# Gate and up projections as seven block products, ffn tiles in passes of 12 and 10, in a two-layer decoder step

## The chip, the cores and the metric

The kernel runs on one core of one Trainium2 chip. The metric is the device time of one execution in microseconds (us), the median of the runs shown. Engines are PE (TensorE, the matmuls), PEld (its weight loads), DVE (VectorE), ACT (ScalarE), POOL (GpSimd) and SP (SyncE, which issues loads).

## The reference

One step of a decoder of two layers over 520 tokens (a prompt of 512 and eight sequences of one new token), all in fp32. Each layer has a mixer (layer 0 gated linear recurrence and pooling, layer 1 retention), a residual add, and the feed-forward network (ffn) that this case is about; a last norm follows. D_MODEL is 1024, D_FF 2816.

```python
def rms_norm(x, gain=None):
    y = x32 * lax.rsqrt(jnp.mean(x32 * x32, axis=-1, keepdims=True) + EPS)
    ...
def swiglu(h, w_gate, w_up, w_down):
    return (jax.nn.silu(h @ w_gate) * (h @ w_up)) @ w_down
...
        x = x + y
        x = x + swiglu(rms_norm(x, norm_ffn[i]), w_ffn_gate[i], w_ffn_up[i], w_ffn_down[i])
    return rms_norm(x, norm_final), ...
```

## The kernel before

Activations lie transposed: `x` is 128 partitions by 8 k-tiles by 520 tokens, and every projection makes one 128x520 tile of outputs in PSUM, as two halves of 260 tokens. TensorE multiplies in a rounded fp32 format, so each fp32 factor is split into a rounded part (hi) and the rest (lo), and a product is three matmuls: hi times hi, hi times lo and lo times hi. ScalarE makes hi by a copy with rounding (`hi` L351, `h_hi` L360), VectorE makes lo by a subtraction (`lo` L706, `h_lo` L711).

Per layer the ffn has 22 tiles of 128 hidden units. Each tile is one load of 1 MB (weights of gate and up, 128x2048), and two products of 48 matmuls (8 k-tiles, 3 splits, 2 halves), gate and up, through two alternating PSUM tiles `ps`. VectorE evicts both with a multiplication by `rstd`, the rms-norm's factor per token (L722 into `t0` and `t2`); ScalarE makes silu (L476); VectorE multiplies (L958), makes the next weights' lo (L706) and the lo of the hidden tile (L961); ScalarE its hi (L480). After all 22 come eight down tiles of 132 matmuls (two loads of 11 k-tiles each), added to `x` by one VectorE instruction each (`residual`, L722). In layer 0 each is followed by `h_lo` (L711) for the next projection. The squares for the next norm are GpSimd's (L1236, L1238); TensorE sums them over partitions (`norm_sum`, L1379) and spreads the factor (`norm_spread`, L1387), in the first tile of the phase that follows.

The order on each engine is written out by hand, in one program for each, tied by counting semaphores: `wait_ge(s, n)` holds an engine's queue until a count is reached. The long stretches are hardware loops over two tiles. SP loads a chunk when the hi and lo of two chunks before are done.

The last down tile of the kernel runs half by half (L1862), 66 matmuls each, and the final norm of the first half (`last_squares`, `y_sum` L1843, `y_spread` L1852, six outputs L1214) is put inside and behind the second:

```python
                    if t == 1 and n == Y_AFTER[0]:
                        y_sum(0)
                    if t == 1 and n == Y_AFTER[1]:
                        y_spread(0)
```

## Time and profile before

| | before |
|---|---|
| median of 3 runs | 1501.72 us (1501.26 to 1503.73) |
| profiled execution, span | 1500.0 us |
| PE busy | 1469.1 us (98%), 11754 matmuls |
| DVE busy | 728.8 us (49%) |
| ACT busy | 475.5 us (32%) |
| POOL busy | 208.4 us (14%) |
| share of the chain that ended last: PE, DVE | 95%, 2% |

The span is one execution by the hardware profiler, from its first instruction to its last. A time in the chain is a stretch of work that nothing but itself held up. "Idle" is the time an engine stood still ahead of an instruction, with what released it.

### The profile page before, as it was taken

What the parts mean: (1) busy time and instruction counts of PE and PEld (TensorE: products, weight loads), DVE (VectorE), ACT (ScalarE), POOL (GpSimd) and SP (SyncE); (2) the same over time, 40 slices, a digit from 0 to 9 for tenths busy, and PEclk for the clock granted to TensorE, in tenths of its full rate; (3) what the DMA queues carried; (4) which work ended last, traced back from release to release, by engine and by line L of the source; (5) the groups of instructions that cost most, each with busy time, mean ns of one, the idle gap of its engine ahead of it and who ended that gap; (6) DMA issues with size and microseconds to landing.
All of it is one profiled execution on the core that took longest, in us unless ns stands there. A gap on an engine that the chain in (4) does not pass through costs nothing.

```text
span 1500.0 us, 28016 instructions
## 1 busy us (share of the span) xinstructions
PE 1469.1 (98%) x11754; PEld 1426.6 (95%) x11754; DVE 728.8 (49%) x867; ACT 475.5 (32%) x547; POOL 208.4 (14%) x209
## 2 busy tenths in 40 slices
PE   6999999999999999999999999989999999999997
PEld 5989999999999999988989989979999999999997
DVE  6564544444443333465574773875444444443223
ACT  3432232222222212254263362463222222221111
POOL 6011130000000112014013041041210000000221
PEclk9999999999999999999999999999999999999998
DMA  6212122222222222555254263333222222222221
GB/s 236 85 61 93 54 88 85 84 97 99 84 75 77 95 97 90 219 175 183 85 204 154 98 232 111 140 140 142 85 99 99 84 84 98 97 66 78 96 97 57
DMA packets 32230, 165.84 MB, mean 111 GB/s; under 512 B 3904, under 2 KB 6224, under 8 KB 20400
## 3 DMA queue, kind: packets, MB, share of 16 engines
q1 hardware_dynamic: 21792, 126.90, 24.3%
q0 software_dynamic: 10384, 38.16, 7.1%
q8 instruction: 40, 0.66, 0.2%
q14 instruction: 14, 0.11, 0.0%
HBM read 140.46 MB, written 24.59 MB: 110 GB/s over the span
## 4 chain that ended last, share of the span: by engine, by line
PE 95%; DVE 2%; ACT 1%; POOL 1%; issue 0%; DMA 0%; DVEq 0%; SPq 0%; ACTq 0%; POOLq 0%
PE ps L1361 83%; PE ax L1722 2%; PE ax L1731 1%; PE ax L1704 1%; PE ps L1862 1%; PE ax L1651 1%; PE ax L1743 1%; PE ax L1379 1%; PE ax L1387 1%; DVE h_lo L711 1%; PE ax L1689 0%; PE ax L1530 0%; POOL acc L1233 0%; PE ax L1499 0%; DMA x<-in_x 0%
## 5 line engine op out<-in xcount | busy, mean ns | idle before, releaser
L1361 PE MATMUL ps<-h_hi,whi 128*128 128x260 f32 x2432 | 496.8, 285 | 1.3 <-DVE wlo L731 1.3
L1361 PE MATMUL ps<-h_hi,wlo 128*128 128x260 f32 x2432 | 491.1, 284 | 0.0
L1361 PE MATMUL ps<-h_lo,whi 128*128 128x260 f32 x2432 | 490.1, 283 | 0.0
L1361 PEld LDWEIGHTS ps<-h_hi,whi 128*128 128x128 f32 x2432 | 376.4, 189 | 8.0 <-issue 4.9
L1361 PEld LDWEIGHTS ps<-h_hi,wlo 128*128 128x128 f32 x2432 | 375.9, 189 | 0.0
L1361 PEld LDWEIGHTS ps<-h_lo,whi 128*128 128x128 f32 x2432 | 375.4, 189 | 0.0
L351 ACT ACTIVATE whi<-raw 128x2048 fp32r<-128x2048 f32 (+1 forms) x119 | 210.6, 1770 | 490.4 <-PE ps L1361 481.9
L706 DVE TENSOR_TENSOR wlo<-raw,whi 128x2048 fp32r<-128x2048 f32 (+1 forms) x119 | 255.5, 2147 | 128.9 <-ACT whi L351 128.7
L722 DVE TENSOR_TENSOR t<-ps,rstd 128x520 f32<-128x520 f32 x108 | 75.5, 699 | 274.8 <-PE ps L1361 269.1
L1361 PE MATMUL ps<-hid_hi,whi 128*128 128x260 f32 x660 | 133.2, 283 | 0.0
L1361 PE MATMUL ps<-hid_hi,wlo 128*128 128x260 f32 x660 | 132.7, 282 | 0.0
L1361 PE MATMUL ps<-hid_lo,whi 128*128 128x260 f32 x660 | 132.6, 282 | 0.0
L1361 PEld LDWEIGHTS ps<-hid_lo,whi 128*128 128x128 f32 x660 | 101.9, 188 | 0.0
L1361 PEld LDWEIGHTS ps<-hid_hi,wlo 128*128 128x128 f32 x660 | 101.7, 188 | 0.0
L1361 PEld LDWEIGHTS ps<-hid_hi,whi 128*128 128x128 f32 x660 | 101.6, 188 | 0.0
L1229 POOL TENSOR_TENSOR acc<-x 128x520 f32<-128x520 f32 x5 | 5.8, 1162 | 593.2 <-DVE x L722 538.9
L476 ACT ACTIVATE t<-t 128x520 f32<-128x520 f32 x44 | 28.2, 640 | 171.9 <-DVE t L722 171.9
L722 DVE TENSOR_TENSOR x<-ps,x 128x520 f32 (+1 forms) x31 | 21.7, 699 | 120.6 <-PE ps L1361 120.4
L1236 POOL TENSOR_TENSOR sq<-x 128x520 f32<-128x520 f32 x32 | 35.7, 1114 | 242.2 <-DVE x L722 241.5
L360 ACT ACTIVATE h_hi<-x,vec 128x520 fp32r<-128x520 f32 (+1 forms) x32 | 22.7, 726 | 126.5 <-DVE x L722 124.9
L1238 POOL TENSOR_TENSOR acc<-acc,sq 128x520 f32<-128x520 f32 x32 | 61.0, 1907 | 2.5
L1361 PE MATMUL ps<-o_hi,whi 128*128 128x260 f32 x256 | 52.7, 288 | 6.6 <-issue 2.9
(260 smaller groups left out, 1587.6 us busy)
## 6 DMA issues: line engine op xcount, KB each, us to landing
raw<-in_w_f SPq DMA_DIRECT2D x44, 1024.0 KB, 4.7
...
```

The costliest lines, as they stand in the source:

```text
L351: act.activation(whi[slot][:, 0:size], raw[slot][:, 0:size], ACT.Copy).then_inc(s_whi, 1)
L360: act.activation(flat(h[0], m), flat(x, m), ACT.Copy, scale=gain(n, m)).then_inc(s_hhi, 1)
L476: act.activation(t1[:], t0[:], ACT.Silu).then_inc(s_sg, 1)
L706: dve.tensor_tensor(wlo[slot][:, 0:size], raw[slot][:, 0:size], whi[slot][:, 0:size].bitcast(F32), ALU.subtract).then_inc(s_wlo, 1)
L711: dve.scalar_tensor_tensor(out=flat(h[1], m), in0=flat(x, m), scalar=gain(n, m), in1=flat(h[0], m).bitcast(F32), op0=ALU.mult, op1=ALU.sub ...
L722: dve.tensor_tensor(out, ps[par][:, :, 0:HT], two(rstd) if other is None else other, op).then_inc(s_out, 1)
L1236: pool.tensor_tensor(sq[:], x[:, m, :], x[:, m, :], ALU.mult).then_inc(s_sq, 1)
L1238: pool.tensor_tensor(acc[:], acc[:], sq[:], ALU.add).then_inc(s_acc, 1)
L1361: ins = pe.matmul(dst[t], lhs(a, kw), rhs[b][:, kx, HT * t:HT * t + HT], start=(first and n == 0 and q == 0), stop=(last and n == len(ks_) ...
L1379: ins = pe.matmul(ax[3][:, col + i:col + i + 1], src[:, a:a + P], ones[:, 0:1], start=True, stop=True)
L1387: ins = pe.matmul(dst, rr[:, rcol + i:rcol + i + 1].to_broadcast([P, P]), ident[:, c:c + n], start=True, stop=True)
L1722: ins = pe.matmul(ax[q % 2][:, P * j:NP_], v[:, j, P * q:P * q + P], p_[:, PROB_AT[j]:PROB_AT[j + 1]], start=(j == 0 and n == 0), stop=(j ...
```

## The change

Gate and up of one ffn tile are now a product of a 2x2 matrix of blocks with another: the rows are up (first) and gate (second), the columns of the right factor are the two halves of 260 tokens, and the inner dimension is cut into the even and the odd k-tiles. Winograd's form of Strassen's scheme needs seven block products for it, of four k-tiles, three splits and one half each, 12 matmuls (`f_product`), so 84 matmuls a tile. It needs four sums of weight blocks (S1 to S4, per tile) and four of activations (T1 to T4, once per layer, in `hx`, split into `hs`), and seven additions behind the products, of which TensorE's accumulation in PSUM does some. The sums of a tile:

- VectorE: `f_sum_13` (S1 and S3, 128x1024), `f_sum_2` (128x512), `f_sum_4` (128x512), lo of three parts (1536, 1024, 1024), `up_first`, `up_second`, `gate_second` (128x260 each, from PSUM), `gate_first_scaled` and `gate_second_scaled` (128x260, by rstd with the sign), `hidden` and `hid_low` (128x520).
- ScalarE: hi of the same three parts (1536, 1024, 1024), three copies of 128x260 out of PSUM, silu, the hidden tile's hi.

rstd is applied to gate alone ahead of silu; up's factor is left to the down projection, whose tiles are evicted by two instructions (`down_taken`: a multiplication by rstd, L1249, and the add to `x`, L1252, with other VectorE work, `inside`, between). The hidden tensor holds 12 tiles in place of 22, so the ffn has two passes: 12 tiles and eight down tiles of 72 matmuls, then 10 tiles and eight of 60. The sums and splits of `hx` are built pair by pair in the out-projection ahead of the ffn. `norm_sum` stands behind P6 and `norm_spread` behind P7 of the first tile. The last down tile has 30 matmuls a half. Some semaphores of loads and of heads share a number with others now.

```diff
-W_FULL, W_HALF, W_DOWN = 2048, 1024, 11 * P
+W_FULL, W_HALF = 2048, 1024
+FH = (12, 10)
+W_DOWN = (FH[0] * P, FH[1] * P)
+F0 = (0, FH[0])
...
+A11, A12, A22, S1, S2, S3, S4 = range(7)
+F_BLOCK = ({A22: 0, A11: 1, A12: 2, S4: 4, S2: 5, S1: 6, S3: 7}, {A12: 1, A11: 2, A22: 3, S2: 4, S4: 5, S3: 6, S1: 7})
+
+F_RAW = ({"A22": 0, "A11": 1, "A12": 2, "A21": 3}, {"A21": 0, "A12": 1, "A11": 2, "A22": 3})
+B11, T1, B21, B22, T2, T3, T4 = range(7)
...
+            def f_hi_s24(g, q, free):
+                act.wait_ge(f_s4, g + 1)
+                act.wait_ge(*free)
+                act.activation(fw[0][:, 4:6, :], fraw[q][:, raw_sums(q), :], ACT.Copy).then_inc(s_whi, 1)
+
...
+                def period(n, q, first=False, final=False):
+                    f_hi_s24(g0 + n, q, (s_mm, before) if first else (f_p3, g0 + n))
+                    if first and half == 0:
+                        act.wait_ge(s_tlo, 12 * (l + 1))
+                    copies_1(n, q)
+                    if first and half == 0:
+                        copies_5(n, q)
+                        copies_6(n, q)
+                        act.wait_ge(s_ms, 2 * l + 2)
+                        act.activation(rt[:, 0:5], ax[3][:, 64:69], ACT.Sqrt, bias=eps[:, 0:1]).then_inc(s_rt, 1)
+                    if final:
+                        act.wait_ge(f_p2, g0 + n + 1)
+                        hi(cd, 0, W_DOWN[half], (f_p4, g0 + n))
+                    else:
+                        f_hi_raw(g0 + n + 1, 1 - q, c0 + n + 1,
+                                 [(f_p2, g0 + n + 1)] + ([] if first else [(f_p4, g0 + n)]))
+                    if not (first and half == 0):
+                        copies_6(n, q)
+                    if not first:
+                        silu(n - 1, 1 - q)
+                    if not (first and half == 0):
+                        copies_5(n, q)
+                    else:
+                        act.wait_ge(s_bc, 2 * l + 2)
+                        act.activation(rstd[:, 0:NP_], ax[2][:], ACT.Copy)
+                        act.activation(rstd[:, NP_:T], ax[3][:, 72:72 + NS], ACT.Copy).then_inc(s_rstd, 1)
+                    if not first:
+                        hid_high(n - 1)
+                    if not final:
+                        f_hi_s13(g0 + n + 1, (f_p7, g0 + n + 1))
+
+                if half == 1:
+                    f_hi_s13(g0, (s_mm, before))
...
+            def hx_sum(sn, j, part):
+
+                n = 4 * sn + j
+                if part == 0:
+                    dve.wait_ge(s_hx, 2 * n + 1)
+                    dve.tensor_tensor(hx[:, T1, :], hx[:, B11, :], hx[:, 7, :], ALU.subtract).then_inc(s_tsum, 1)
+                else:
+                    dve.wait_ge(s_hx, 2 * n + 2)
+                    dve.tensor_tensor(hx[:, T3, :], hx[:, B22, :], hx[:, 7, :], ALU.subtract).then_inc(s_tsum, 1)
+                    dve.wait_ge(s_tsum, 4 * n + 1)
+                    dve.scalar_tensor_tensor(out=hx[:, T2, :], in0=hx[:, B22, :], scalar=-1.0, in1=hx[:, T1, :],
+                                             op0=ALU.mult, op1=ALU.subtract).then_inc(s_tsum, 1)
+                    dve.wait_ge(s_tsum, 4 * n + 3)
+                    dve.scalar_tensor_tensor(out=hx[:, T4, :], in0=hx[:, T2, :], scalar=-1.0, in1=hx[:, B21, :],
+                                             op0=ALU.mult, op1=ALU.subtract).then_inc(s_tsum, 1)
...
+            def f_lo_raw(g, q):
+                dve.wait_ge(f_ha, g + 1)
+                a = raw_triple(q)
+                dve.tensor_tensor(fw[1][:, a, :], fraw[q][:, a, :], fw[0][:, a, :].bitcast(F32), ALU.subtract).then_inc(f_la, 1)
+
...
+                def period(n, q, first=False, final=False):
+                    if not (first and half == 0):
+                        f_lo_s13(g0 + n)
+                    if not first:
+                        up_second(n - 1, 1 - q)
+                    f_lo_s24(q, c0 + n)
+                    if not final:
+                        f_sum_13(g0 + n + 1, 1 - q, c0 + n + 1)
+                        f_sum_2(g0 + n + 1, 1 - q)
+                    if not first:
+                        gate_first_scaled(n - 1, 1 - q)
+                    up_first(n, q)
+                    if first and half == 0:
+                        invert(2 * l + 1)
+                    if final:
+                        lo(cd, 0, W_DOWN[half])
+                    else:
+                        f_lo_raw(g0 + n + 1, 1 - q)
+                        f_sum_4(g0 + n + 1, 1 - q)
+                    if not first:
+                        hidden(n - 1, 1 - q)
+                    gate_second(n, q)
+                    if not first:
+                        hid_low(n - 1)
+                    if first and half == 0:
+                        dve.wait_ge(s_rstd, 2 * l + 2)
+                    gate_second_scaled(n, q)
...
+            def down_taken(l, half, m, q, inside):
+
+                dm = M_D[l][half]
+                dve.wait_ge(s_mm, dm + m + 1)
+                want(dve, s_xd, 16 * l + 8 * half + m)
+                dve.tensor_tensor(two(t1), ps[(dm + q) % 2][:, :, 0:HT], two(rstd), ALU.mult).then_inc(s_out, 1)
+                inside()
+                dve.wait_ge(s_out, dm + m + 1)
+                dve.tensor_tensor(flat(x, m), t1[:], flat(x, m), ALU.add).then_inc(s_xd, 1)
...
+                def tile_(m, q):
+                    down_taken(l, half, m, q, lambda: lo(d0 + m + 2, q, size))
+                    if (l, half) == (0, 1):
+                        h_lo(2, m)
...
+                if half == 0:
+                    def first_sums():
+                        f_sum_13(g1, 0, C_F[l][1])
+                        f_sum_2(g1, 0)
+
+                    def first_raw():
+                        f_lo_raw(g1, 0)
+                        f_sum_4(g1, 0)
+
+                    down_taken(l, half, 6, 0, first_sums)
+                    down_taken(l, half, 7, 1, first_raw)
+                elif l == 0:
+                    for m in (6, 7):
+                        down_taken(l, half, m, m % 2, lambda: lo(C_OI + m - 6, m - 6, W_FULL))
+                        h_lo(2, m)
+                else:
...
+                def f_product(block, moving, bank, start, done, ready=None):
+
+                    for j in range(4):
+                        if ready is not None:
+                            pe.wait_ge(s_tlo, 12 * l + 3 * j + ready)
+                        for n, (a, b) in enumerate(((0, 0), (0, 1), (1, 0))):
+                            ins = pe.matmul(bank, fw[a][:, block, P * j:P * j + P], hs[b][:, j, moving, :],
+                                            start=(start and j == 0 and n == 0), stop=(j == 3 and n == 2),
+                                            skip_group_check=True)
+                    ins.then_inc(done, 1)
+
+                def product_4(n, q):
+                    pe.wait_ge(f_g1, g0 + n + 1)
+                    f_product(F_BLOCK[q][A22], T4, bank_a(q), False, f_p4)
...
+                def chunk(n, q, first=False):
+                    blocks, g = F_BLOCK[q], g0 + n
+                    early = first and half == 0
+
+                    def product_5():
+                        pe.wait_ge(f_lb, g + 1)
+                        want(pe, f_u1, g - 1)
+                        f_product(blocks[S1], T1, bank_d(q), True, f_p5, 1 if early else None)
+
+                    pe.wait_ge(f_la, g + 1)
+                    if first:
+                        pe.wait_ge(s_out, before - 1)
+                    want(pe, f_gr, 2 * g - 2)
+                    f_product(blocks[A11], B11, bank_a(q), True, f_p1, 1 if early else None)
+                    if early:
+                        product_5()
+                    want(pe, f_u0, g - 1)
+                    f_product(blocks[A12], B21, bank_e(q), True, f_p2, 2 if early else None)
+                    if not first:
+                        product_4(n - 1, 1 - q)
+                    pe.wait_ge(s_wlo, c0 + n + 1)
+                    pe.wait_ge(f_k1, g + 1)
+                    f_product(blocks[S2], T2, bank_a(q), False, f_p6, 3 if early else None)
+                    if early:
+                        norm_sum(2 * l + 1)
+                    else:
+                        product_5()
+                    pe.wait_ge(f_k6, g + 1)
+                    f_product(blocks[S3], T3, bank_a(q), False, f_p7)
+                    if early:
+                        norm_spread(2 * l + 1)
+                    pe.wait_ge(f_k5, g + 1)
+                    f_product(blocks[S4], B22, bank_d(q), False, f_p3)
+
+                chunk(0, 0, first=True)
+                pe.wait_ge(s_out, before)
+                with pe.Fori(0, last // 2) as i:
+                    chunk(2 * i + 1, 1)
+                    chunk(2 * i + 2, 0)
+                chunk(last, 1)
...
-                for n in range(FT):
-                    if n % 11 == 0:
-                        pe.wait_ge(s_wlo, C_D[1] + N_D - 1 + n // 11)
+                for n in range(FH[1]):```

VectorE's queue in the loop over gate/up tiles, before: one tile (t_62 to t_65 are t0 to t3, the number behind wlo, raw and whi is a buffer; what is waited for stands in brackets).

```order
L721 ISA [waits silu_gate]
L722 TENSOR_TENSOR t_62<-ps,rstd 128x520 [waits mtile_done]
L721 REGISTER_ALU
L722 TENSOR_TENSOR t_64<-ps,rstd 128x520 [waits mtile_done]
L956 REGISTER_ALU [waits mtile_taken]
L958 TENSOR_TENSOR t_65<-t_64,t_63 128x520 [waits hidden_hi,silu_gate]
L705 REGISTER_ALU
L706 TENSOR_TENSOR wlo_53<-raw_49,whi_51 128x2048 [waits weights_hi]
L961 ISA [waits hidden_hi]
L961 TENSOR_TENSOR hid_lo<-t_65,hid_hi 128x520
```

The same queue and place in the change: the last ten of one tile's thirteen instructions, behind L1137, L1176 and L1141 (f_lo of S1 and S3, `up_second`, f_lo of S2 and S4).

```order
L1115 TENSOR_TENSOR f_sum<-f_raw_75 128x1024 [waits ffn_s1_s3_lo,raw1_loaded]
L1120 REGISTER_ALU
L1121 TENSOR_TENSOR f_raw_75<-f_sum,f_raw_75 128x512 [waits ffn_s1_s3_summed]
L1191 SCALAR_TENSOR_TENSOR rs<-ps,rstd 128x260 [waits ffn_product4]
L1171 TENSOR_TENSOR t_64<-ax,t_64 128x260 [waits ffn_product1_copied,ffn_product2]
L1133 TENSOR_TENSOR f_lo<-f_raw_75,f_hi 128x1536 [waits ffn_raw_hi]
L1128 TENSOR_TENSOR f_raw_75<-f_raw_75 128x512 [waits ffn_raw_lo]
L1199 TENSOR_TENSOR t_65<-t_63,sq 128x520 [waits ffn_up_second,hidden_hi,ffn_up_first,silu_gate]
L1181 TENSOR_TENSOR t_62<-ps,t_62 128x260 [waits ffn_product5_copied,ffn_product7]
L1203 ISA [waits hidden_hi]
L1203 TENSOR_TENSOR hid_lo<-t_65,hid_hi 128x520
L1186 SCALAR_TENSOR_TENSOR t_62<-t_62,rstd 128x260 [waits ffn_gate_second]
```

Five instructions of a tile became thirteen. L1121 and L1128 wait for the instruction that stands right ahead of them; L1203 waits for ScalarE's copy of what L1199 made, two instructions before.

VectorE's queue at the end of the first pass, in the change: the last two down tiles of it and the first weights of the second pass. There is no such place before.

```order
L1249 TENSOR_TENSOR t_63<-ps,rstd 128x520 [waits x_after_down,mtile_done]
L1115 TENSOR_TENSOR f_sum<-f_raw_74 128x1024 [waits ffn_s1_s3_lo,raw0_loaded]
L1121 TENSOR_TENSOR f_raw_74<-f_sum,f_raw_74 128x512 [waits ffn_s1_s3_summed]
L1252 TENSOR_TENSOR x<-t_63,x 128x520 [waits mtile_taken]
L1249 TENSOR_TENSOR t_63<-ps,rstd 128x520 [waits x_after_down,mtile_done]
L1133 TENSOR_TENSOR f_lo<-f_raw_74,f_hi 128x1536 [waits ffn_raw_hi]
L1128 TENSOR_TENSOR f_raw_74<-f_raw_74 128x512 [waits ffn_raw_lo]
L1252 TENSOR_TENSOR x<-t_63,x 128x520 [waits mtile_taken]
L1137 TENSOR_TENSOR f_lo<-f_sum,f_hi 128x1024 [waits ffn_s1_s3_hi]
L1141 TENSOR_TENSOR f_lo<-f_raw_74,f_hi 128x1024 [waits weights_hi]
```

The lo that the second pass's first product needs (L1133) stands behind the eviction of the pass's last down tile (the second L1249).

VectorE's queue at the end of layer 0, before: the last down tile, with weights for layer 1's projection around it.

```order
L706 TENSOR_TENSOR wlo_53<-raw_49,whi_51 128x2048 [waits weights_hi]
L722 TENSOR_TENSOR x<-ps,x 128x520 [waits mtile_done]
L711 SCALAR_TENSOR_TENSOR h_lo<-x,vec,h_hi 128x520 [waits h_hi_written]
L706 TENSOR_TENSOR wlo_54<-raw_50,whi_52 128x2048 [waits weights_hi]
L717 RECIPROCAL rr<-rt 128x5 [waits rms]
```

The same place in the change.

```order
L1249 TENSOR_TENSOR t_63<-ps,rstd 128x520 [waits x_after_down,mtile_done]
L864 TENSOR_TENSOR wlo_54<-raw_50,whi_52 128x2048 [waits weights_hi]
L1252 TENSOR_TENSOR x<-t_63,x 128x520 [waits mtile_taken]
L869 SCALAR_TENSOR_TENSOR h_lo<-x,vec,h_hi 128x520 [waits h_hi_written]
L875 RECIPROCAL rr<-rt 128x5 [waits rms]
```

The lo of the second weight buffer (128x2048) has moved from behind the residual add and `h_lo` to between the eviction and the add.

## Rows read from the trace of the kernel before

**Rows 1.** The page, busy time of each engine: us, share of the span, instructions.

```profile
PE 1469.1 (98%) x11754; PEld 1426.6 (95%) x11754; DVE 728.8 (49%) x867; ACT 475.5 (32%) x547; POOL 208.4 (14%) x209
```

**Rows 2.** The chain that ended last: start us, duration us, engine, tile, line, instructions.

```profile
220.53 375.00 PE ps L1361 x3120
...
1111.82 359.08 PE ps L1361 x2988
1470.90 9.77 PE ps L1862 x81
...
1490.49 0.85 PE ax L1852 x6
```

**Rows 3.** Windows: us, busy of PE, PEld, DVE, ACT, POOL (instructions), PE clock, DMA share, GB/s.

```profile
222.00:590.00 368.00, 368.00 (x3065) 368.00 (x3064) 147.05 (x138) 93.09 (x89) 15.74 (x13) 1.00 0.26 89
```

**Rows 4.** Timeline of DVE in the gate/up loop: start us, duration us, instruction [idle before].

```profile
307.18 0.70 DVE L722 TENSOR_TENSOR t<-ps,rstd 128x520 f32<-128x520 f32 x1 [5.07 <-PE ps L1361]
308.07 0.70 DVE L958 TENSOR_TENSOR t<-t,t 128x520 f32<-128x520 f32 x1 [0.19 <-DVE t L722]
309.13 2.29 DVE L706 TENSOR_TENSOR wlo<-raw,whi 128x2048 fp32r<-128x2048 f32 x1 [0.36 <-ACT whi L351]
311.34 0.69 DVE L961 TENSOR_TENSOR hid_lo<-t,hid_hi 128x520 f32 x1
```

**Rows 5.** Groups of instructions by line and shape: busy us, mean ns | idle before.

```profile
L706 DVE TENSOR_TENSOR wlo<-raw,whi 128x2048 fp32r<-128x2048 f32 x87 | 200.5, 2305 | 52.6 <-ACT whi L351 52.6
L351 ACT ACTIVATE whi<-raw 128x2048 fp32r<-128x2048 f32 x87 | 166.6, 1914 | 347.4 <-PE ps L1361 338.8 <-DMA raw<-in_w_oi 7.7 <-DMA raw<-in_w_e 0.8
...
L480 ACT ACTIVATE hid_hi<-t 128x520 f32 x36 | 22.3, 619 | 0.0
...
L360 ACT ACTIVATE h_hi<-x,vec 128x520 fp32r<-128x520 f32 x17 | 11.9, 726 | 39.5 <-DVE x L722 37.8 <-DMA x<-in_x 1.6
...
L1124 DVE SCALAR_TENSOR_TENSOR ktok_lo<-ax,vec,ktok_hi 128x256 fp32r<-128x256 f32 x16 | 6.6, 476 | 0.0
```

**Rows 6.** Timeline of DVE and POOL in layer 1's out-projection.

```profile
1071.41 2.29 DVE L706 TENSOR_TENSOR wlo<-raw,whi 128x2048 fp32r<-128x2048 f32 x1 [1.13 <-ACT whi L351]
...
1071.48 3.38 POOL L1238 TENSOR_TENSOR acc<-acc,sq 128x520 f32<-128x520 f32 x1
...
1105.91 1.31 POOL L1238 TENSOR_TENSOR acc<-acc,sq 128x520 f32<-128x520 f32 x1
```

**Rows 7.** Timeline at layer 0's first gate/up tile, DVE, POOL and PE.

```profile
212.38 0.70 DVE L722 TENSOR_TENSOR x<-ps,x 128x520 f32<-128x520 f32 x1 [3.38 <-PE ps L1361]
...
214.29 1.65 POOL L1238 TENSOR_TENSOR acc<-acc,sq 128x520 f32<-128x520 f32 x1
...
215.99 1.17 PE L1379 MATMUL ax<-ones,acc 128*128 128x1 f32 x9
```

**Rows 8.** Timeline at layer 0's end: DVE, PE.

```profile
595.56 0.70 DVE L722 TENSOR_TENSOR x<-ps,x 128x520 f32<-128x520 f32 x1 [3.63 <-PE ps L1361]
...
599.17 1.05 PE L1379 MATMUL ax<-ones,acc 128*128 128x1 f32 x8
```

**Rows 9.** Timeline of the kernel's tail: DVE.

```profile
1484.25 3.43 DVE L1214 SCALAR_TENSOR_TENSOR x<-x,vec,rstd 128x256 f32<-128x256 f32 x6 [2.30 <-ACT rstd L694]
1488.14 0.43 DVE L1202 TENSOR_TENSOR x<-ps,x 128x260 f32<-128x260 f32 x1 [0.47 <-PE ps L1862]
1488.61 0.43 DVE L1206 TENSOR_TENSOR sq<-x 128x260 f32<-128x260 f32 x1
...
1491.85 3.58 DVE L1214 SCALAR_TENSOR_TENSOR x<-x,vec,rstd 128x264 f32<-128x264 f32 x6 [1.41 <-ACT rstd L699]
```

**Rows 10.** Windows behind layer 1's mixer, columns as in group 3.

```profile
1001.00:1004.00 3.00, 1.60 (x9) 1.43 (x10) 2.90 (x4) 1.17 (x3) 1.06 (x2) 0.89 0.43 173
1004.00:1007.00 3.00, 3.00 (x13) 2.63 (x12) 0.00 (x0) 1.04 (x3) 0.00 (x0) 0.54 0.02 7
```

**Rows 11.** Timeline of PE there: start us, duration us, instruction [idle before].

```profile
1002.18 0.47 PE L1361 MATMUL ps<-o_hi,whi 128*128 128x260 f32 x2 [2.94 <-issue]
```

More of the change, by code:

```diff
@@ L305, in _ @@
             phase(C_EO, N_EO, io["w_eo"], W_FULL)
-            phase(C_F[0], N_F, io["w_f0"], W_FULL)
-            phase(C_D[0], N_D, io["w_d0"], W_DOWN)
+            for half in range(2):
+                phase(C_F[0][half], FH[half], io["w_f0"], W_FULL, base=F0[half], ffn=True)
+                phase(C_D[0][half], N_D, io[f"w_d0{half}"], W_DOWN[half])
             for j in range(2):
@@ L325, in _ @@
             phase(C_OO, N_OO, io["w_oo"], W_FULL, 4)
-            phase(C_F[1], N_F, io["w_f1"], W_FULL)
-            phase(C_D[1], N_D, io["w_d1"], W_DOWN)
+            for half in range(2):
+                phase(C_F[1][half], FH[half], io["w_f1"], W_FULL, base=F0[half], ffn=True)
+                phase(C_D[1][half], N_D, io[f"w_d1{half}"], W_DOWN[half])
             for part, (a, b, _) in enumerate(Y_PARTS):
@@ L499, in _ @@
+            def ffn(l):
+                for half in range(2):
+                    gate_up(l, half)
+                    down(l, half)
             ffn(0)
@@ new lines, in down_ready, with before, down, tile_ @@
+            def down_ready(l, half):
+                def before(k):
+                    pe.wait_ge(s_hidlo, FT * l + F0[half] + k + 1)
+                return before
+            def down(l, half):
+                d0, dm, n = C_D[l][half], M_D[l][half], FH[half]
+                g = FT * l + F0[half] + n
+                def tile_(m, q, before=None):
+                    pe.wait_ge(s_wlo, d0 + m + 1)
+                    product(dm + m, (dm + q) % 2, [(k, k) for k in range(n)], weights(q, 0, P), (hid_hi, hid_lo),
+                            True, True, before=before)
+                pe.wait_ge(f_gr, 2 * g - 2)
+                pe.wait_ge(f_u1, g - 1)
+                tile_(0, 0, down_ready(l, half))
+                pe.wait_ge(f_gr, 2 * g)
+                pe.wait_ge(f_u1, g)
+                tile_(1, 1)
+                with pe.Fori(1, 3) as i:
+                    for q in range(2):
+                        tile_(2 * i + q, q)
+                tile_(6, 0)
+                if (l, half) != (1, 1):
+                    tile_(7, 1)
@@ L1640, in _ @@
+            def ffn(l):
+                for half in range(2):
+                    gate_up(l, half)
+                    down(l, half)
             ffn(0)
```

648 lines of the change are left out of this document (395 added, 253 removed).

## The prediction

> **What bounds the kernel now.** The page's first lines say that TensorE is busy for 98% of the span and VectorE for 49% [rows 1]. The chain that ended last says where that can be used: two stretches of matmuls, each held up by nothing but itself, take 375.00 us for 3120 matmuls and 359.08 us for 2988 [rows 2], 0.1202 us each. They are the two ffns, and the granted clock over 222 to 590 us is 1.00 [rows 3]. So in the ffn a matmul less is 0.12 us less, as long as the other engines keep up; the loop's timeline shows VectorE idle for 5.07 us ahead of an eviction [rows 4]. The busy shares do not show what the change would ask of VectorE; that has to be counted.
>
> I compare one execution with another: the profiled one took 1500.0 us, 1.7 below the median of 1501.72, and I add 1.7 at the end.
>
> **What it removes.** 44 tiles lose 12 matmuls each: 528 x 0.1202 = 63.5 us. A tile is 84 x 0.1202 = 10.10 us in place of 11.54. That a weight is used by one 260-column matmul and not by two in a row costs nothing that I can see: the last down tile already runs so, 81 in 9.77 us, 0.1206 each [rows 2], and the page has as many weight loads as matmuls [rows 1]. The down tiles have the same matmuls in all. Loads are the same bytes.
>
> **What it adds in each tile.** VectorE's 13 instructions. A tensor-tensor of 520 takes 0.70 us and one of 2048 takes 2.29 [rows 4], that is 0.159 us and 1.041 ns per element. So 3 x 1024 are 3.68, 1536 is 1.76, 2 x 512 are 1.38, 2 x 520 are 1.40, 3 x 260 are 1.29; the two scalar-tensor-tensors of 260 I take at 0.48 (256 elements took 476 ns [rows 5]). Sum 10.47 us of durations, already more than TensorE's 10.10.
>
> Two things move it. L961, which waited for nothing late, starts at 311.34, while L706 ends at 309.13 + 2.29 = 311.42 [rows 4]: an instruction whose inputs are there starts 0.08 before the end of the one before. Ten of the thirteen starts can be so: -0.80. Two (`f_sum_2`, `f_sum_4`) wait for the instruction right ahead; L958, which does the same, starts 0.19 behind it [rows 4]: +0.38. The last, `hid_low`, waits for ScalarE's copy of `hidden` (0.62 [rows 5]), with only `gate_second` (0.43) between. If ScalarE starts at once the gap is about 0.25; if the hand-over shows as much as the idle 0.36 ahead of L706 [rows 4], about 0.3 more, 0.55. Together 10.3 to 10.6; I take **10.45 against 10.10**, so VectorE sets the pace, by 0.35. The first two tiles of each of the four passes start with VectorE ahead, which leaves 36 tiles: 36 x 0.35 = **+12.5 us**. Bounds: 0 if the waits vanish in the loop, and 36 x 1.25 = 45 if no start overlaps (10.47 + 0.38 + 0.5 = 11.35).
>
> The Trainium skill bears on this (VectorE: DVE Perf Modes, "The DRAIN you can't avoid"): the next instruction does not start until the pipe of the one before is empty, semaphore or none, though it allows an earlier start where nothing holds it. Row and rule differ where it is read strictly: L961 started early; by it the +12.5 would be +45.
>
> ScalarE's part, by 1.91 for 2048 and 0.62 for 520 [rows 5], is 1536 (1.49), 2 x 1024 (1.05 each), three copies of 260 (about 0.41), 0.64 and 0.62: 6.1 us a tile, below 10.1, so hidden, though each copy is waited for by a product.
>
> **The first tile of each layer.** TensorE cannot start P5, P2 and P6 until the last pair of `hx` is summed and split. After the out-projection's last tile VectorE evicts x (0.70), ScalarE makes hi of S1 and S3 (1.05, beside it) and the scaled x (0.73 [rows 5]), VectorE then lo (1.22), T3, T2, T4 (0.43 + 0.48 + 0.48), lo of 520 and of 780 (0.70, 0.97; the second waits for a ScalarE copy of 0.83 behind T4) and lo of S2 and S4 (1.22): P6 can start 6.85 us after that tile, against 4.33 for three products of 1.44. With the wait for the squares ahead of `norm_sum`, the spread behind P7, and the second tile's lo, the tile loses about 5 in layer 1. In layer 0 the weight sums of tile 0 (1.22 + 0.69 + 1.76 + 0.69 = 4.4) stand in the pair before, which VectorE takes into the last pair: 7.5. GpSimd makes it worse: its accumulation takes 1.31 alone and 3.38 beside a VectorE subtraction that starts with it [rows 6]. Before, x was there at 213.08 and `norm_sum` ran at 215.99 [rows 7], inside a tile's matmuls. Sum **+12.5**; bounds 7.4 (both layers with the waits alone) and 18.
>
> **The turn between the passes, twice.** P1 of the second pass waits for `f_lo_raw`, queued behind the last down tile's eviction: 0.2 to see TensorE's end, 0.70, then 1.76, with 0.2 to TensorE, less the overlap: 2.85. P6 waits for lo of S2 and S4, four instructions further (0.69 + 0.70 + 1.22 + 1.22 and a ScalarE copy): 0.75 more. 3.6 each, **+7.2** (5.7 to 9).
>
> **Layer 0's end.** The lo of 2048 for the next phase now stands between eviction and add. It waits for ScalarE's hi (1.91, free only when the down tile ends), takes 2.29, and the add comes behind it: x(7) is ready 4.9 after the tile instead of 0.7 [rows 8]. The squares and `norm_sum` at 599.17 followed x without slack, and `h_lo` comes behind it too: **+4.2** (2 to 5).
>
> **The tail.** Before, from the last tile's start at 1470.90 to the end, 29.1; with 72 matmuls less 20.4 would do. Now `y_spread(0)` stands at the tile's end, 8.05 after its start (60 matmuls and `y_sum`), and the six outputs of part 0 (3.43) come behind it and ahead of the second half's squares: 8.05 + 0.75 + 0.45 + 3.43 + three instructions 1.3 = 14.0, and from the squares' end at 1489.04 to 1500.0 [rows 9] is 11.0: 25.0, so **+4.6** (2 to 5). The spread's price is 0.85 at most [rows 2].
>
> **The clock.** After 2.94 us of idle ahead of a matmul at 1002.18 [rows 11] the granted clock was 0.89 and then, over 1004 to 1007, 0.54 [rows 10], which is near the lower level of 1.2 GHz; the two windows lost 3 x 0.11 + 3 x 0.46 = 1.7 us by it. The turns (2.85, twice) and layer 0's end (4.2) make idle stretches like it: **+3** (0 to 5).
>
> Sum: -63.5 + 12.5 + 12.5 + 7.2 + 4.2 + 4.6 + 3 = -19.5; 1480.5, and with 1.7 about **1482**.
>
> **Rivals.** (a) TensorE keeps the pace: the dependent waits shrink to what unrolled code would show, and only the joints cost. 1482 - 12.5 = 1469.5, less if the first tiles come at their lower bound: 1461 to 1471. For it: the margin of 0.35 us is a sum over thirteen small terms; against it: 10.47 of durations. (b) VectorE pays more per tile than I take, 10.7 to 10.9: 1491 to 1498. (c) Slower: in this loop no start overlaps, because most instructions wait for a semaphore of another engine: 11.35 a tile, 1482 + 32.5 = 1514.5. It decides from 10.10 + (63.5 - 31.5) / 36 = 10.99 us a tile. For it: two of the loop's four starts before came late (0.19, 0.36); against it: those waited for work just ended, and L961's early start. The strict rule of the Trainium skill (same page and section) is this rival. (d) A single product is slower than 84 x 0.1202, since accumulation goes on in one bank: the last tile's 0.1206 speaks against it, and I give it nothing.
>
> **How the numbers follow.** My forecast (10.3 to 10.6 a tile, 1473 to 1491) gets 0.54, (a) 0.18, (b) 0.12, (c) 0.12, and 0.04 is for a sum that ends within 0.2%, about what a measurement of this kernel can tell from no change. Faster is 0.54 + 0.18 + 0.12 = 0.84, slower 0.12. The range leaves out half of (a)'s low end and (c): 1463 to 1500.
>
> **What would show it.** Loop tiles of 10.45 us on TensorE with a wait in each for VectorE's lo or sums; VectorE busy about 95% in the ffn and without long idle; 2.9 us ahead of P1 at both turns; 4.2 us of TensorE idle at layer 0's end; part 0's six outputs ahead of the second half's eviction in the tail. Tiles of 10.10 would make it (a), of more than 11 (c). I am wrong in a way that I don't see if the stretch between the joints is neither.

## The result, and the profile after

The changed kernel takes 1483.97 us (median of 4 runs, 1481.04 to 1485.15) against 1501.53 of the kernel before in the same runs. The ratio is 0.9875, with a 95% interval of 0.9862 to 0.9887: 1.25% faster. The profiled execution has a span of 1479.5 us, 20.5 below the one before; the prediction was 19.5 below and 1482.

The page's busy line answers to [rows 1].

```profile
PE 1424.0 (96%) x11226; PEld 1377.2 (93%) x11226; DVE 984.7 (67%) x1308; ACT 627.9 (42%) x809; POOL 194.6 (13%) x209
```

TensorE has 528 matmuls less, as it should, but it is busy for 96% in place of 98%, and VectorE has gone from 49% to 67%. Shares do not say where the time went, so I cut both traces at the same five places (the end of each out-projection, of layer 0's ffn, and the start of the last down tile).

| stretch, us | before | after | what the matmuls alone would change | left over |
|---|---|---|---|---|
| up to the end of layer 0's out-projection | 212.2 | 211.9 | 0 | -0.3 |
| layer 0's ffn | 383.3 | 367.9 | -31.7 | +16.3 |
| layer 1's mixer | 508.2 | 515.4 | 0 | +7.2 |
| layer 1's ffn without its last down tile | 367.2 | 358.5 | -31.7 + 8.7 | +14.3 |
| last down tile and tail | 29.1 | 25.8 | -8.7 | +5.4 |
| sum | 1500.0 | 1479.5 | -63.4 | +42.9 |

(264 matmuls of a layer are 31.7 us at 0.1202; the last tile has 72 less, which the other down tiles got.) The gain is whole and 42.9 us are lost again. The chain that ended last shows how differently the two passes of layer 0 run; its columns are those of [rows 2].

```profile
270.09 1.68 DVE f_lo L1133
...
291.23 1.68 DVE f_lo L1133
...
423.66 7.47 PE ps L1940 x60
431.13 1.45 PE ax L1940 x12
432.58 8.64 PE ps L1940 x72
```

In the second pass (from 423.66) it is matmuls alone, 72 + 12 in 10.09 us: the 10.10 of the prediction (its last three tiles take 10.2). In the first pass the chain runs through VectorE, and the same instruction comes every 21.14 us (291.23 - 270.09), two tiles of 10.57. VectorE runs the same thirteen instructions in both passes, so they alone cannot be the reason. VectorE's timeline there, columns as in [rows 4], first pass and then second:

```profile
295.23 0.70 DVE L1203 TENSOR_TENSOR hid_lo<-t,hid_hi 128x520 f32 x1 [0.65 <-ACT hid_hi L579]
295.84 0.42 DVE L1186 SCALAR_TENSOR_TENSOR t<-t,rstd 128x260 f32<-128x260 f32 x1
...
298.43 1.23 DVE L1141 TENSOR_TENSOR f_lo<-f_raw,f_hi 128x1024 fp32r<-128x1024 f32 x1 [0.69 <-ACT f_hi L539]
299.57 1.22 DVE L1115 TENSOR_TENSOR f_sum<-f_raw 128x1024 f32<-128x1024 f32 x1
300.82 0.69 DVE L1121 TENSOR_TENSOR f_raw<-f_sum,f_raw 128x512 f32<-128x512 f32 x1
...
470.34 0.70 DVE L1203 TENSOR_TENSOR hid_lo<-t,hid_hi 128x520 f32 x1 [0.68 <-ACT hid_hi L579]
...
471.30 1.22 DVE L1137 TENSOR_TENSOR f_lo<-f_sum,f_hi 128x1024 fp32r<-128x1024 f32 x1
...
481.47 1.22 DVE L1137 TENSOR_TENSOR f_lo<-f_sum,f_hi 128x1024 fp32r<-128x1024 f32 x1
```

The second pass has one idle stretch per tile, 0.65 to 0.68 ahead of L1203, and a tile is 10.17 (481.47 - 471.30; over the pass 10.17 to 10.22). The first pass has a second one in every other tile: L1141 waits 0.69 for ScalarE's hi (L539). ScalarE's timeline there says why:

```profile
296.04 1.28 ACT L539 ACT_TABLE_LOAD   x1
297.34 1.06 ACT L539 ACTIVATE f_hi<-f_raw 128x1024 fp32r<-128x1024 f32 x1
...
301.85 1.28 ACT L574 ACT_TABLE_LOAD   x1
303.14 0.65 ACT L574 ACTIVATE t<-t 128x520 f32<-128x520 f32 x1
```

There is a load of a function table in the loop, ahead of a copy, and another ahead of silu. The groups by line count them: ten each, two for each of the five rounds of the two first passes, and none in the second passes. The third line is the kernel before: there silu's load comes once a layer, in the first tile, ahead of the loop.

```profile
L539 ACT ACT_TABLE_LOAD x10 | 12.8, 1283 | 0.9 <-DVE f_raw L1128 0.8
L574 ACT ACT_TABLE_LOAD x10 | 12.8, 1283 | 0.2
...
L476 ACT ACT_TABLE_LOAD x2 | 2.6, 1283 | 0.0
```

In the change the first tile holds the square root of the norm, and its silu has moved into the second tile, which is in the loop. So the loop of a first pass begins with another table than it ends with; the loop of a second pass begins and ends with silu's. The prediction did not look for that. That this is why the loads stand there is tested in e1.

The turn between the passes and layer 0's end, DVE and PE, the latter answering to [rows 8]:

```profile
417.63 0.70 DVE L1249 TENSOR_TENSOR t<-ps,rstd 128x520 f32<-128x520 f32 x1 [5.44 <-PE ps L1685]
418.25 1.75 DVE L1133 TENSOR_TENSOR f_lo<-f_raw,f_hi 128x1536 fp32r<-128x1536 f32 x1
...
420.05 0.39 PE L1940 MATMUL ps<-hs_hi,f_hi 128*128 128x260 f32 x1 [2.46 <-DVE f_lo L1133]
423.66 0.39 PE L1940 MATMUL ps<-hs_hi,f_hi 128*128 128x260 f32 x1 [0.46 <-DVE f_lo L1141]
...
579.86 0.70 DVE L1249 TENSOR_TENSOR t<-ps,rstd 128x520 f32<-128x520 f32 x1 [0.58 <-PE ps L1685]
581.88 2.29 DVE L864 TENSOR_TENSOR wlo<-raw,whi 128x2048 fp32r<-128x2048 f32 x1 [1.32 <-ACT whi L397]
584.08 0.69 DVE L1252 TENSOR_TENSOR x<-t,x 128x520 f32<-128x520 f32 x1
...
587.65 2.29 PE L1703 MATMUL ax<-ones,acc 128*128 128x1 f32 x10 [4.25 <-POOL acc L1560]
```

Both are as the prediction drew them: the lo behind the eviction at the turn, and the add of x(7) behind a 2.29 us subtraction at layer 0's end, with TensorE idle for 4.25. The second pass takes 104.6 us from 417.6 to 522.3 for 101.0 of matmuls, so a turn costs 3.7, with some 0.3 of it in the last three tiles. At layer 0's end TensorE also runs at a granted clock of 0.50, the lower of its two levels, 1.2 GHz (columns as in [rows 3]):

```profile
588.00:590.00 2.00, 2.00 (x11) 2.00 (x11) 0.00 (x0) 0.01 (x1) 2.00 (x5) 0.50 0.98 399
```

The same matmuls from `norm_sum` to the loop take 7.04 us there (587.65 to 594.69) and took 4.55 before (599.17 to 603.72): 2.5 us.

The tail, answering to [rows 9]:

```profile
1462.71 3.40 DVE L1536 SCALAR_TENSOR_TENSOR x<-x,vec,rstd 128x256 f32<-128x256 f32 x6 [2.31 <-ACT rstd L852]
1466.03 0.42 DVE L1523 TENSOR_TENSOR t<-ps,rstd 128x260 f32<-128x260 f32 x1
```

The second half's eviction (L1523) waits behind the six outputs of part 0, without idle between. And the first tile of layer 0: PE, then VectorE and GpSimd.

```profile
213.90 0.36 PE L1940 MATMUL ps<-hs_hi,f_hi 128*128 128x260 f32 x1 [2.02 <-issue]
...
224.92 0.39 PE L1940 MATMUL ps<-hs_hi,f_hi 128*128 128x260 f32 x1 [0.62 <-DVE f_lo L1141]
...
218.59 1.27 DVE L1095 TENSOR_TENSOR hx<-hx 128x260 f32<-128x260 f32 x1
219.79 1.52 DVE L1097 SCALAR_TENSOR_TENSOR hx<-hx 128x260 f32<-128x260 f32 x1
221.34 0.43 DVE L1100 SCALAR_TENSOR_TENSOR hx<-hx 128x260 f32<-128x260 f32 x1
...
217.62 1.96 POOL L1558 TENSOR_TENSOR sq<-x 128x520 f32<-128x520 f32 x1 [1.25 <-DVE x L880]
219.66 1.36 POOL L1560 TENSOR_TENSOR acc<-acc,sq 128x520 f32<-128x520 f32 x1
```

P6 begins at 224.92 (the second PE line; the first is P1), 13.0 us behind the out-projection (211.9), where three products need 4.3. The sums T3 and T2 (L1095, L1097) take 1.27 and 1.52 us beside GpSimd's two instructions, T4 (L1100) 0.43 once GpSimd is done.

### The profile page after: what moved, and what is told of

The parts are those of the page before. It is cut to its first block, busy times and chain, and to the rows that moved or that the text cites. A ratio compares the mean times of both kernels' runs of the same rounds, so it can differ in the third digit from the quotient of the medians.

```text
span 1479.5 us, 28114 instructions
## 1 busy us (share of the span) xinstructions
PE 1424.0 (96%) x11226; PEld 1377.2 (93%) x11226; DVE 984.7 (67%) x1308; ACT 627.9 (42%) x809; POOL 194.6 (13%) x209
## 4 chain that ended last, share of the span: by engine, by line
PE 80%; DVE 11%; ACT 5%; issue 3%; DMA 0%; ACTq 0%; DVEq 0%; POOL 0%; SPq 0%
PE ps L1685 49%; PE ps L1940 16%; PE ax L1940 2%; PE ax L2106 2%; PE ax L2115 2%; DVE f_lo L1141 2%; DVE f_lo L1133 1%; PE ax L2088 1%; PE ax L2035 1%; DVE f_lo L1137 1%; PE ax L2127 1%; PE ax L1703 1%; PE ax L1711 1%; DVE h_lo L869 1%; DVE f_sum L1115 1%
## 5 line engine op out<-in xcount | busy, mean ns | idle before, releaser
L1940 PE MATMUL ps<-hs_hi,f_hi 128*128 128x260 f32 x1056 | 304.3, 288 | 18.3 <-DVE f_lo L1141 7.8
L1940 PE MATMUL ps<-hs_lo,f_hi 128*128 128x260 f32 x1056 | 300.4, 284 | 0.0
L1940 PE MATMUL ps<-hs_hi,f_lo 128*128 128x260 f32 x1056 | 300.2, 284 | 0.0
L397 ACT ACTIVATE whi<-raw 128x2048 fp32r<-128x2048 f32 (+2 forms) x75 | 126.4, 1685 | 301.4 <-PE ps L1685 292.9
L1940 PEld LDWEIGHTS ps<-hs_hi,f_hi 128*128 128x128 f32 x1056 | 200.5, 190 | 23.1 <-DVE f_lo L1141 10.4
L1685 PE MATMUL ps<-h_hi,whi 128*128 128x260 f32 x1024 | 214.4, 291 | 1.3 <-DVE wlo L889 1.2
L1685 PE MATMUL ps<-h_lo,whi 128*128 128x260 f32 x1024 | 208.1, 285 | 0.0
L1685 PE MATMUL ps<-h_hi,wlo 128*128 128x260 f32 x1024 | 208.0, 285 | 0.0
L1940 PEld LDWEIGHTS ps<-hs_lo,f_hi 128*128 128x128 f32 x1056 | 201.0, 190 | 0.0
L1940 PEld LDWEIGHTS ps<-hs_hi,f_lo 128*128 128x128 f32 x1056 | 200.7, 190 | 0.0
L864 DVE TENSOR_TENSOR wlo<-raw,whi 128x2048 fp32r<-128x2048 f32 (+2 forms) x75 | 153.7, 2050 | 49.9 <-ACT whi L397 49.9
L1685 PEld LDWEIGHTS ps<-h_hi,whi 128*128 128x128 f32 x1024 | 160.2, 191 | 7.7 <-issue 5.3
L1685 PEld LDWEIGHTS ps<-h_lo,whi 128*128 128x128 f32 x1024 | 160.3, 191 | 0.0
L1685 PEld LDWEIGHTS ps<-h_hi,wlo 128*128 128x128 f32 x1024 | 159.8, 191 | 0.0
L1685 PE MATMUL ps<-hid_lo,whi 128*128 128x260 f32 x684 | 137.7, 283 | 0.0
L1685 PE MATMUL ps<-hid_hi,whi 128*128 128x260 f32 x684 | 137.6, 282 | 0.0
L1685 PE MATMUL ps<-hid_hi,wlo 128*128 128x260 f32 x684 | 137.3, 282 | 0.0
L1685 PEld LDWEIGHTS ps<-hid_lo,whi 128*128 128x128 f32 x684 | 105.4, 188 | 0.0
L1685 PEld LDWEIGHTS ps<-hid_hi,wlo 128*128 128x128 f32 x684 | 105.3, 188 | 0.0
L1685 PEld LDWEIGHTS ps<-hid_hi,whi 128*128 128x128 f32 x684 | 105.2, 188 | 0.0
```

The source lines that it names most:

```text
L397: act.activation(whi[slot][:, 0:size], raw[slot][:, 0:size], ACT.Copy).then_inc(s_whi, 1)
L864: dve.tensor_tensor(wlo[slot][:, 0:size], raw[slot][:, 0:size], whi[slot][:, 0:size].bitcast(F32), ALU.subtract).then_inc(s_wlo, 1)
L1685: ins = pe.matmul(dst[t], lhs(a, kw), rhs[b][:, kx, HT * t:HT * t + HT], start=(first and n == 0 and q == 0), stop=(last and n == len(ks_) ...
L1940: ins = pe.matmul(bank, fw[a][:, block, P * j:P * j + P], hs[b][:, j, moving, :], start=(start and j == 0 and n == 0), stop=(j == 3 and n ...
```

## The experiments

Theory 1 after the result: the first passes lose 8 us to table loads, not to VectorE's thirteen instructions; the rest of the loss sits in the joints (first tiles, turns, layer 0's end, tail), each with a queue order as its cause. The rival is the prediction's own: VectorE at 10.45 a tile. Ratios below are to the kernel before, measured beside each version.

**e1: a Silu ahead of the loop.** One instruction on eight columns that nobody reads.

```diff
                     if not final:
                         f_hi_s13(g0 + n + 1, (f_p7, g0 + n + 1))
+                    if first and half == 0:
+                        act.activation(rt[:, 8:16], eps[:], ACT.Silu)
```

> One Silu on eight columns that nobody reads, put behind the first tile of each layer, so that ScalarE's function table is Silu's when the loop of the first pass begins. Theory 1 (the first passes are slow by the 20 table loads of 1.28 us that stand in their loops): no load is left in a loop, the tiles of the first passes go from 10.57 to 10.1 or 10.2 us, and the kernel gains 2 x 10 x 0.38 = 7 to 8 us, 1476. Theory 2 (VectorE's thirteen instructions alone set the pace there, as the prediction had it): tiles stay at 10.5, no gain.

Measured: 1477.43 us (ratio to the kernel before 0.9829, 0.9809 to 0.9848). ScalarE's timeline in the loop has no load any more, and the chain of the first pass is matmuls.

```profile
293.39 1.05 ACT L539 ACTIVATE f_hi<-f_raw 128x1024 fp32r<-128x1024 f32 x1
...
298.57 0.64 ACT L574 ACTIVATE t<-t 128x520 f32<-128x520 f32 x1
...
244.46 8.64 PE ps L1942 x72
...
254.55 8.64 PE ps L1942 x72
...
305.31 8.72 PE ps L1942 x72
...
315.48 8.72 PE ps L1942 x72
```

Tiles are 10.09 us at first (254.55 - 244.46) and 10.17 later (315.48 - 305.31). From the second tile to the end of the first pass, 936 matmuls or 112.5 us, the change takes 116.7 and 116.3 us in the two layers and this kernel 113.3 and 113.4: 6.3 us of the 8.0 are gone, and the medians differ by 6.5, a little under the 7 to 8 expected. Theory 1 holds for these 6.3, and 10.45 a tile is out. The 1.7 that are left are tiles of 10.17, VectorE's pace, as e3 shows.

**e2 and e3: VectorE's limit from both sides.** On top of e1, one VectorE instruction more per tile (the diff leaves out its calls, and that the eviction of P4 now stands behind `up_first`), or two made short (of those two sums most is left out; `up_second` is shortened like the one shown).

```diff
# e2
+                def gate_first_extra(n, q):
+                    dve.wait_ge(f_p4, g0 + n + 1)
+                    dve.scalar_tensor_tensor(out=gate[q][:, 0:HT], in0=bank_a(q), scalar=-1.0, in1=rstd[:, 0:HT],
+                                             op0=ALU.mult, op1=ALU.mult).then_inc(f_x, 1)
# e3
-                    dve.tensor_tensor(up[q][:, 0:HT], bank_e(q), up[q][:, 0:HT], ALU.add).then_inc(f_u0, 1)
+                    dve.tensor_tensor(up[q][:, 0:8], bank_e(q)[:, 0:8], up[q][:, 0:8], ALU.add).then_inc(f_u0, 1)
```

> The kernel of the Silu experiment with one VectorE instruction of 260 elements more in every tile (the scaled eviction of P4 done twice). If VectorE is at its limit without it (its instructions stand 10.17 to 10.21 us apart from tile to tile), each tile becomes 10.5 us in both passes: 36 x 0.34 = 12 us above the Silu experiment, less what slack the second passes begin with. If TensorE sets the pace with room to spare on VectorE, the tiles stay at 10.1.

> The kernel of the Silu experiment with the two additions of up's products done on 8 columns in place of 260 (most of two sums is left out). Some 0.5 us less of VectorE per tile, a cycle of 9.7. If VectorE holds the first passes at 10.19, they go to TensorE's 10.09: 2 us less than the Silu experiment. If it is not VectorE but a chain through ScalarE and the copies, nothing changes.

Measured, one run each: 1482.92 and 1473.73 us. VectorE's timeline of e2 in the second pass:

```profile
466.34 1.75 DVE L1135 TENSOR_TENSOR f_lo<-f_raw,f_hi 128x1536 fp32r<-128x1536 f32 x1
...
476.89 1.75 DVE L1135 TENSOR_TENSOR f_lo<-f_raw,f_hi 128x1536 fp32r<-128x1536 f32 x1
```

Tiles are 10.55 and 10.51 in turn there, and 10.51 in the first pass: the instruction's 0.34 us comes through in full. The two passes cost 3.4 and 2.3 us more than in e1 in layer 0, 3.4 and 1.5 in layer 1: 10.6 of the 12 expected. The time rose by only 5.5: in e2's execution layer 1's first tile (from the out-projection to P1 of the second) took 15.0 us and not 18.2, at a granted clock of 1.00, and the stretch ahead of layer 0's ffn 1.0 less; the rest is not accounted for. In e3 the loop's tiles are 10.09, and the first pass takes 112.7 for its 112.5. So VectorE's limit is 10.17, with the wait of 0.65 for ScalarE's copy in it, just above TensorE's 10.10: 0.07 us, a fifth of one short instruction, decides who sets the pace.

**e4: three joints in another order.** The change itself, without e1 (ScalarE's copies at layer 0's end, left out here, are reordered to match).

```diff
                     down_taken(l, half, 6, 0, first_sums)
-                    down_taken(l, half, 7, 1, first_raw)
+                    first_raw()
+                    down_taken(l, half, 7, 1, lambda: None)
...
-                    for m in (6, 7):
-                        down_taken(l, half, m, m % 2, lambda: lo(C_OI + m - 6, m - 6, W_FULL))
-                        h_lo(2, m)
+                    down_taken(l, half, 6, 0, lambda: lo(C_OI, 0, W_FULL))
+                    h_lo(2, 6)
+                    down_taken(l, half, 7, 1, lambda: None)
+                    h_lo(2, 7)
+                    lo(C_OI + 1, 1, W_FULL)
...
+            last_squares(0, 0, HT)
+            y_invert(0)
+            last_squares(1, HT, T)
+            y_outputs(0, Y_DVE[:3])
+            y_invert(1)
+            y_outputs(0, Y_DVE[3:])
+            y_outputs(1, Y_DVE)
```

> The change with three places reordered, nothing else. At the turn between the passes f_lo_raw and f_sum_4 stand ahead of the last down tile's eviction: if the queue order there is what costs, the wait of 2.9 and 0.75 us ahead of P1 and P6 becomes about 1.2 in all, twice -2.4. At layer 0's end the lo of 2048 stands behind the add and h_lo: norm_sum comes 3.8 us after the last down tile and not 7.8, -4, and up to 2.6 more if the low clock there goes. In the tail the second half's squares and its reciprocal stand ahead of part 0's outputs: 25.8 us from the last tile's start to the end become 22.3. Sum -12 to -15, 1469 to 1472. Rival: what waits there is held by something else as well (a copy of ScalarE, the squares of GpSimd), and less than half of it comes.

Measured: 1467.89 us (0.9765, 0.9744 to 0.9787). Its TensorE timeline at the turn and at layer 0's end:

```profile
424.60 0.39 PE L1955 MATMUL ps<-hs_hi,f_hi 128*128 128x260 f32 x1 [0.92 <-DVE f_lo L1142]
...
585.17 1.28 PE L1718 MATMUL ax<-ones,acc 128*128 128x1 f32 x10 [0.78 <-POOL acc L1575]
```

P1 waits for nothing, P6 for 0.92, and a second pass takes 102.4 in place of 104.6: 2.2 each. `norm_sum` comes 4.4 us behind the last down tile in place of 7.8. The tail is 21.8 us from the last tile's start (1448.39, span 1470.2) in place of 25.8. That is 2 x 2.2 + 3.4 + 4.0 = 11.8. The clock stays up at layer 0's end,

```profile
588.00:592.00 4.00, 4.00 (x36) 4.00 (x36) 1.55 (x3) 0.67 (x2) 0.00 (x0) 1.00 1.06 336
```

and from `norm_sum` to the loop the matmuls take 4.55 again and not 7.04: 2.5 more, 14.3 in all. The medians are 16.1 apart, a little over the 12 to 15 expected. Queue order is the cause at all three.

**e7 and e6: all of it together, and two moves more.** e7 is e1 with e4. e6 also puts the lo of S1, S3, S2 and S4 ahead of the last add at the turn, and in layer 0's out-projection moves `f_lo_raw` and `f_sum_4` behind the eviction of tile 6 (the second move is shown):

```diff
                 residual(m, m % 2, 2 * n)
+                if n == N_EO - 1:
+                    f_lo_raw(0, 0)
+                    f_sum_4(0, 0)
                 hx_sum(0, n, 0)
...
                     f_sum_2(0, 0)
-                    f_lo_raw(0, 0)
-                    f_sum_4(0, 0)
```

> The Silu experiment and the three reordered places, without the two further moves. Sum of the single ones: 1484 - 7 - 12 = 1465; the stretches of the trace are to show the same values as in the two experiments apart: first passes at 10.1 to 10.2 us a tile, 2.4 us less at each turn, 3.4 less at layer 0's end, 4.0 less in the tail.

> The Silu experiment and the three reordered places together, with two more moves: at the turn the lo of S1 and S3 and of S2 and S4 stand between the last eviction and its add (P6's wait 0.5 instead of 1.2), and in layer 0's out-projection f_lo_raw and f_sum_4 of the first tile stand behind the eviction of tile 6 instead of ahead of it (P1 of layer 0 waits for that eviction; it should come 2.4 us earlier, and P1 be held by f_lo_raw instead: its wait of 2.0 becomes about 1.4, and the low clock of the 10 us behind it may go or stay). If the terms add up: 1484 - 7 (table loads) - 5 (turns) - 4 (layer 0's end) - 4 (tail) = 1464, and 1460 if the clock stays up at layer 0's first tile. If the gains hide one another, 1468 or more.

Measured: e7 1464.09 us (0.9746, 0.9731 to 0.9761), e6 1464.01 (0.9744, 0.973 to 0.9757). The terms add up. The two further moves together brought nothing that can be told. At the turn P6 waits 0.73 in place of 0.92 (0.5 was expected), and the second pass is 0.2 shorter than in e7. At layer 0's first tile e6 loses 0.4: P1 of the second tile comes 20.5 us behind the out-projection and not 20.1. P1 of the first tile begins after a wait of 1.25 in place of 2.02, but its own last k-tile then waits 2.94 for T1's lo (`hs_lo`), where it waited 1.06 in the change. That k-tile starts 5.5 us behind the out-projection in e6 (221.52 after 215.99) and 5.1 in the change (216.99 after 211.88): VectorE's work was moved, not made less.

**e8: TensorE kept busy in the first tiles.** On top of e7, matmuls of `ident` with itself into a bank that nobody reads, ahead of P1, P5 and P6 (the calls ahead of P5 and P6 are left out).

```diff
+                def keep_busy(n):
+                    for _ in range(n):
+                        pe.matmul(ax[2][:, 0:P], ident[:], ident[:], start=True, stop=True)
...
+                    if early and l == 0:
+                        keep_busy(16)
                     pe.wait_ge(f_la, g + 1)
```

> The Silu experiment and the three reordered places, and TensorE given matmuls of 128x128 into a bank that nobody reads, where it stands still in the first tile of each layer: 16, 4 and 4 of them ahead of P1, P5 and P6 in layer 0, 12 and 14 ahead of P5 and P6 in layer 1. Theory 1 (the first tiles cost more than predicted because TensorE's granted clock falls to 0.5 behind the idle there): with the clock at 1.00 through the first tiles, layer 0's takes 16 us from the out-projection's end to its P3 instead of 20, and layer 1's 16 instead of 18; 4 to 6 us less, 1459, and less spread. Theory 2 (the clock falls for another reason, or VectorE's chain sets the end of the tile anyway): the waits for VectorE grow by what the matmuls gain, and less than 2 us come.

Measured: 1462.2 us (0.9726, 0.9704 to 0.9747), not to be told from e7. A window of the change at layer 0's first tile, then two of e8, columns as in [rows 3]:

```profile
222.00:224.00 2.00, 2.00 (x11) 1.99 (x10) 1.69 (x3) 1.91 (x4) 0.00 (x0) 0.50 0.00 0
```

```profile
216.00:220.00 4.00, 3.53 (x31) 3.33 (x30) 2.50 (x4) 2.32 (x3) 2.43 (x2) 1.00 0.00 0
224.00:228.00 4.00, 2.12 (x16) 1.77 (x15) 3.69 (x5) 2.47 (x4) 0.00 (x0) 1.00 0.00 0
```

The granted clock stays at 1.00, and yet the stretch from the out-projection's end to P1 of the second tile is 20.1 us (214.5 to 234.59) where the change has 20.1 (211.9 to 231.94), and P6 comes 13.1 and 13.0 behind the out-projection: in layer 0 the low clock costs nothing as the queues stand, VectorE's chain to P6 sets the end. That is theory 2. In layer 1 the added matmuls stood in the way: P5 began 3.9 us after the out-projection in place of 3.0, and `norm_sum` came 11.4 us after it in place of 9.9.

**e9: GpSimd's last square held back.** On top of e7.

```diff
-                squares(1, m, (s_out, M_EO + m + 1))
+                squares(1, m, (s_out, M_EO + m + 1) if m < 7 else (s_wlo, C_F[0][0] + 1))
```

(and the same for layer 1)

> The Silu experiment and the three reordered places, with GpSimd's square of the last x tile ahead of each ffn held back until VectorE has made the lo of S2 and S4 of the first tile. If GpSimd's two instructions are what makes the sums of hx take 1.3 to 1.5 us there instead of 0.43, T3 and T2 take 0.43 to 0.5 each, P6 starts 1.5 to 2 us earlier in each layer, and norm_sum then waits about 1 us for the square: 1 to 2 us less in all, 1462 to 1463. If not, the durations stay and norm_sum comes 2 us later: slower by 2 to 4.

Measured: 1462.21 us (0.9738, 0.972 to 0.9755), not to be told from e7. VectorE's timeline and GpSimd's effect on TensorE in layer 0:

```profile
221.11 0.42 DVE L1098 TENSOR_TENSOR hx<-hx 128x260 f32<-128x260 f32 x1
221.45 0.42 DVE L1100 SCALAR_TENSOR_TENSOR hx<-hx 128x260 f32<-128x260 f32 x1
...
229.21 1.38 PE L1720 MATMUL ax<-ones,acc 128*128 128x1 f32 x10 [0.90 <-POOL acc L1577]
```

T3 and T2 take 0.42 each, so the 1.27 and 1.52 were GpSimd's doing. P6 comes 12.2 us behind layer 0's out-projection in place of 13.0, and 6.7 behind layer 1's in place of 8.4; 1.5 to 2 earlier was expected of both. In layer 0 VectorE's lo is ready 11.0 behind, and P5 and P2 at the granted clock of 0.50 hold P6 for the rest: with GpSimd out of the way the low clock does cost there. `norm_sum` then waits 0.90 for GpSimd (2.03 in layer 1). The cost is shown, and that this move only shifts it.

## Why the prediction was right, and where not

The time was right, and in part by luck. The places of the joints were right and most of their prices near; the pace of the loop was 4.5 us too dear and had another cause, and the first tiles 2.7 too cheap. The forecast hung on tiles of 10.3 to 10.6 us by VectorE's pace, and no pass had them: the first passes' 10.57 came of table loads, and the second passes, at 10.09 for most of their tiles, were what the prediction called rival (a).

The measured column takes the stretches of the first table apart; a layer's first tile is what the pace and the turn leave of its ffn.

| term, us | predicted | measured |
|---|---|---|
| 528 matmuls less | -63.5 | -63.5 (84 matmuls in 10.09 in the second passes) |
| pace of the loop | +12.5 | +8.0 (4.2 and 3.8, first passes alone) |
| first tiles | +12.5 (7.5 and 5) | +15.2 (8.4 and 6.8) |
| two turns | +7.2 | +7.4 |
| layer 0's end, and the clock | +4.2, +3 | +7.2 (4.2 of wait, 2.5 of clock, 0.5 elsewhere in layer 1's mixer) |
| tail | +4.6 | +5.4 |
| start | 0 | -0.3 |

- **The pace.** The step "VectorE sets the pace, 10.45 against 10.10, 36 tiles" failed. VectorE's own tile is 10.17: the two dependent sums start 0.03 behind the instruction ahead (L1121 at 300.82 after 299.57 + 1.22), not 0.19 as L958 did; the scalar-tensor-tensors take 0.42 in place of 0.48; the gap ahead of `hid_low` is 0.65 where I had 0.25 to 0.55. At 10.17 the backlog of 0.08 a tile shows only in the last three tiles of a second pass. What cost 6.3 of the 8 us is the 20 table loads, which e1 removes; the other 1.7 are the 10.17. I counted VectorE's queue and took ScalarE's 6.1 us as hidden, with no place in it for a load of 1.28 us. The Trainium skill (ScalarE: Activation LUTs, "Table sets: the hidden batching unit") says to batch activations by table set and not by function; e1 agrees with that at the edge of a loop.
- **The overlap.** Rival (c), no overlap and 11.35 a tile, is out: starts 0.08 ahead of the last end are everywhere in the loop (L1186 at 295.84, L1203 ends 295.93). Here the trace does not agree with the strict reading of the Trainium skill (VectorE: DVE Perf Modes, "The DRAIN you can't avoid"), and does with its clause that an instruction that nothing holds starts earlier.
- **The first tiles.** The chain was drawn rightly, and two terms were put at nothing. GpSimd, named as making it worse but given no price, lengthens T3 and T2 by 0.8 and 1.1 us in layer 0 (in layer 1 the lo ahead of T3 and T3, by 0.5 and 1.1 in e7 against e9); without that (e9) VectorE is ready for P6 11.0 us after layer 0's out-projection, and P6 comes 6.7 after layer 1's, where I had 6.85, in layer 0 with 4.4 of VectorE's backlog. With it P6 comes at 13.0 and 8.4. The other is the clock in layer 1: the stretch from the out-projection to P1 of the second tile takes 18.2 us in the change and 15.0 in e7's profile, where the clock stays up (and in e2's), so some 3.2 of the 6.8. A window of the change there, then one of e7:

```profile
1108.00:1112.00 4.00, 4.00 (x21) 4.00 (x20) 2.79 (x3) 0.90 (x2) 0.00 (x0) 0.51 0.04 16
```

```profile
1096.00:1100.00 4.00, 4.00 (x37) 4.00 (x36) 1.89 (x5) 2.03 (x3) 0.00 (x0) 1.00 0.79 254
```

- **The turns, layer 0's end, the tail** were right in place and within 1 us in price, and e4 shows the order of the queues to be the cause. Of the tail's 5.4 it takes back 4.0; the rest stays open.
- **The clock.** Of the places that I named, layer 0's end lost 2.5 us by it; the turns had 2.46 us of idle and stayed at 1.00 in this profile. The windows with 0.50 are the first tiles, layer 0's end (588 to 590) and the tail.
